# An NSA block with kc/vc projected first and its compression laid between the projection's chunks

## The reference, cut to what matters

```python
h = rms_norm(x, norm_mix[1])
q, kc, vc, ks, vs, kw, vw, gates = split(h @ nsa_w_in)       # 1024, 6 x 256, 48 columns
# compressed branch: blocks of 32 rows every 16 rows, 15 blocks, 4 groups of 64 dims
kcmp = rms_norm(silu(blocks(kc + pos_k) @ w1_k) @ w2_k, kcmp_norm)
vcmp = silu(blocks(vc + pos_v) @ w1_v) @ w2_v
o_cmp = softmax(mask(norm(q) @ kcmp.T * 0.125)) @ vcmp       # q without rope here
# two more attentions with rope(norm(q)), over (ks, vs) and (kw, vw)
x = x + (gate0 * o_cmp + gate1 * o_sel + gate2 * o_win) @ nsa_w_out
x = x + memory_cross_attention(rms_norm(x), rms_norm(mem), ...)   # its k and v come from mem
x = x + swiglu(rms_norm(x))
```

## Time and profile before

| | |
|---|---|
| three runs | 1833.73, 1836.98, 1840.62 us, median 1836.98 |
| the profiled execution | 1841.69 us, its span 1840.0 us |
| PE, DVE, ACT, POOL busy over the span | 94%, 62%, 45%, 24% |
| PE clock granted over the span | 0.956 |
| NSA block, projection (445.9 to 508.1 us) | PE full |
| NSA block, 508.1 to 580.7 us | PE granted 0.50 to 1.00 in turns |
| NSA block, attention (580.7 to 659.0 us) | granted 1.00 nearly throughout |

### The profile page before, as it was taken

One profiled execution on the slowest core, in us unless ns is written; L12 is line 12 of the kernel. 1 busy time (PEld: TensorE's weight loads), 2 busy tenths in 40 slices (PEclk: granted clock), 3 DMA queues, 4 the chain that ended last, 5 costly groups with the idle time before them and its releaser, 6 DMA issues. The chain is left out here.

```text
span 1840.0 us, 27212 instructions
## 1 busy us (share of the span) xinstructions
PE 1726.5 (94%) x11063; PEld 1544.7 (84%) x11063; DVE 1144.6 (62%) x1675; ACT 829.4 (45%) x1250; POOL 450.1 (24%) x518
## 2 busy tenths in 40 slices
PE   7899789999988997999999999999999999989998
PEld 5767679987876775999888798799988789879997
DVE  5747556554644756555456875677745787668773
ACT  5434444443432443444344335466534433646652
POOL 1600100001440001000025960224403594223430
PEclk9978899999977998999999899999999999999999
DMA  7501246655520023565655343476556534257652
GB/s 251 179 24 48 93 134 193 183 200 162 195 87 23 24 73 107 144 189 181 203 162 182 115 138 115 115 208 183 184 183 183 160 115 138 92 149 209 185 188 73
DMA packets 293164, 265.58 MB, mean 144 GB/s; under 512 B 18608, under 2 KB 254128, under 8 KB 293040
## 3 DMA queue, kind: packets, MB, share of 16 engines
q1 hardware_dynamic: 293040, 263.85, 46.3%
HBM read 262.78 MB, written 1.05 MB: 143 GB/s over the span
## 5 line engine op out<-in xcount | busy, mean ns | idle before, releaser
L144 DVE TENSOR_TENSOR w_lo<-w_raw,w_hi 128x2048 fp32r<-128x2048 f32 (+1 forms) x246 | 565.4, 2300 | 305.3 <-ACT w_hi L143 299.3
L1506 PE MATMUL bank<-h_hi,w_hi 128*128 128x256 f32 x1984 | 567.1, 286 | 1.8 <-PEq L2029 0.6
L143 ACT ACTIVATE w_hi<-w_raw 128x2048 fp32r<-128x2048 f32 (+1 forms) x246 | 464.8, 1893 | 230.7 <-PE bank L466 128.9
L1507 PE MATMUL bank<-h_lo,w_hi 128*128 128x256 f32 x1984 | 562.6, 284 | 0.0
L1508 PE MATMUL bank<-h_hi,w_lo 128*128 128x256 f32 x1984 | 562.4, 283 | 0.0
L1506 PEld LDWEIGHTS bank<-h_hi,w_hi 128*128 128x128 f32 x1984 | 382.0, 193 | 3.6 <-issue 2.9
L1507 PEld LDWEIGHTS bank<-h_lo,w_hi 128*128 128x128 f32 x1984 | 382.1, 193 | 0.3
L1508 PEld LDWEIGHTS bank<-h_hi,w_lo 128*128 128x128 f32 x1984 | 381.9, 193 | 0.0
L396 PE MATMUL bank<-w_hi,h_hi 128*128 128x512 f32 (+3 forms) x368 | 136.2, 370 | 11.3 <-DVE w_lo L144 6.6
L398 PE MATMUL bank<-w_hi,h_lo 128*128 128x512 f32 (+3 forms) x368 | 135.0, 367 | 0.0
L397 PE MATMUL bank<-w_lo,h_hi 128*128 128x512 f32 (+3 forms) x368 | 134.9, 367 | 0.0
(11 more groups left out here) (431 smaller groups left out, 2972.8 us busy)
## 6 DMA issues: line engine op xcount, KB each, us to landing
w_raw<-in_w_in SPq DMA_DIRECT2D x48, 1024.0 KB, 5.0
w_raw<-in_ffn_w_in SPq DMA_DIRECT2D x88, 512.0 KB, 5.2
w_raw<-in_w_up SPq DMA_DIRECT2D x88, 512.0 KB, 5.2
w_raw<-in_ffn_w_out SPq DMA_DIRECT2D x22, 1024.0 KB, 4.8
w_raw<-in_w_down SPq DMA_DIRECT2D x22, 1024.0 KB, 4.9
w_raw<-in_nsa_w_in SPq DMA_DIRECT2D x10, 1024.0 KB, 5.3
w_raw<-in_ab_w_in SPq DMA_DIRECT2D x8, 1024.0 KB, 8.6
w_raw<-in_mem_w_kv SPq DMA_DIRECT2D x8, 1024.0 KB, 5.2
```

The lines of the kernel that those rows point to most:

```text
L143: return act.activation(hi, raw, ACT.Copy)
L144: return dve.tensor_tensor(self.lo[:, cut_slot, 0:k * n], raw, hi.bitcast(F32), ALU.subtract)
L1506: pe.matmul(out, h, hi[:, f, :], start=(f == 0), stop=False)
L1507: pe.matmul(out, h, lo[:, f, :], start=False, stop=False)
```

## The change

- The projection's blocks are in the order kc/vc, q, q, ks/vs, kw/vw, gates, and the callback `after` on PE comes after each chunk with its number in the block.
- On PE, after the second chunk of block 1: the transposes of kc/vc; after each chunk of block 2: one hidden layer; after the second of block 3: the second layer; after the first of block 4: `turn_q`, after the second: the turn of the compressed keys. ACT's and DVE's counterparts stand in their callbacks of blocks 1 to 4.
- The position vectors are a fifth group of `tokens` (the other columns of it zero), so that the hidden layer has 75 columns and no separate position products. `tokens` lies in the attention's buffers.
- The compressed keys are stored twice with zeros between, so that one score product over all 128 partitions serves two heads: 16 products of 32 columns instead of 32 of 16.
- After the projection: turn of the memory rows into banks 0 to 3, all scores in one bank, memory pieces 0 to 9, transposes of the probabilities, pieces 10 to 15, output products, pieces 16 to 31, feature turn, attention without pieces. The four groups of pieces go to banks 0, 1, 2, 3. The softmax is made once for both row tiles.
- POOL doubles kc/vc first, and makes the compressed key's factor ahead of the third and fourth head norm and of all ropes. The scaling of the kw segment on DVE moves behind the softmax.

The diff, cut to its core (leading blanks shortened; of the queues only the added and unchanged lines, what they replace is in the listing above):

```diff
@@ Project.pe
-            if after is not None:
-                after(pe, j)
+                if after is not None:
+                    after(pe, j, c - self.first[j])
@@ MemoryRows.pe
+            g = i // 8
+            if f == 0 and g >= len(self.sums):
+                pe.wait_ge(self.copied, g - len(self.sums) + 1)
...
+            bank = self.k.bank[self.sums[g % len(self.sums)]][:, :]
@@ nsa_first
-    return [c for col in (0, 512) for c in column_chunks(a["nsa_w_in"], C_W, KD, col, 512)]
+    return [c for col in (C_KC, C_Q) for c in column_chunks(a["nsa_w_in"], C_W, KD, col, 512)]
@@ block_nsa
+tokens = free(k.att[:, :, :, :], [[(NG + 1) * S, 2], [S, NG + 1], [1, S]])
+cmp_pf = [k.exps[:, t, :].rearrange("p (g q) -> p g q", g=NG) for t in range(T)]
+blocks = [(c, c, min(512, C_W - c)) for c in (C_KC, C_Q, C_Q + 512, C_KS, C_KW, C_G)]
@@ gpsimd
+pool.wait_ge(cmp_in, 16 * 5)
+pool.tensor_copy(free(tokens[:, :, :, :], [[(NG + 1) * S, 2], [2, 16]], NG * S), pos_cols[:, :, :])\
+    .then_inc(const, 1)
+pool.wait_ge(project.copied_a, 1)
+pool.wait_ge(project.copied_d, 1)
+copy_twice(pool, scaled, 0, C_KC, ct_doubled)
+copy_twice(pool, scaled, 4, C_VC, ct_doubled)
 pool.wait_ge(gains_in, 16)
 hn.pool(pool, 0)
+mem.features.factors(pool, 2)
 hn.pool(pool, 1)
 pool.wait_ge(ck_stat, 1)
 pool.tensor_scalar(cmp_stat[:, 1:2], cmp_stat[:, 0:1], 1.0 / HD, EPS, ALU.mult, ALU.add)\
     .then_inc(ck_rstd, 1)
 pool.wait_ge(ck_rstd, 1)
 pool.tensor_tensor(cmp_stat[:, 2:3], cmp_stat[:, 1:2], k.minus_half(1), ALU.pow).then_inc(ck_rstd, 1)
+hn.pool(pool, 2)
+pool.wait_ge(turn_q.turned, 4)
+hn.pool_rope(pool, 0)
+hn.pool(pool, 3)
+hn.pool_rope(pool, 1)
+for i in (2, 3):
+    hn.pool_rope(pool, i)
+    pool.wait_ge(hn.turned, hn.turns[i])
+    copy_twice(pool, double[:, :, :, :].rearrange("p t s c -> p t (s c)"), 4 * (i - 2),
+               C_KS if i == 2 else C_KW, doubled)
@@ scalar
+def compress(act, j):
     for i, seg in enumerate(segments):
         if seg[5] == j:
             act.wait_ge(project.copied_a, j + 1)
...
             hn.act(act, i)
     if j == 1:
         mem.act_square(act)
+        for b in range(4):
+            act.wait_ge(ct_turned, b + 1)
+            act.activation(tokens[0:HD, b // 2, 2 * (b % 2):2 * (b % 2) + 2, :],
+                           k.bank[4 + b][0:HD, :].rearrange("p (a b) -> p a b", b=S), ACT.Copy)\
+               .then_inc(ct_low, 1)
+    if j == 2:
+        for i in range(2):
+            act.wait_ge(ch_sum, i + 1)
+            act.activation(cmp_bias[:, i:i + 1], k.bank[HIDDEN[i]][0:HD, NG * N_CMP:NG * N_CMP + 1],
+                           ACT.Copy).then_inc(ch_bias, 1)
+        for i in range(2):
+            act.wait_ge(ch_bias, i + 1)
+            act.wait_ge(const, 7)
+
+            to = hid[0][:, :, 0:N_CMP] if i == 0 else hid[1][:, :, :, 0:N_CMP]
+            of = [[N_CMP, NG], [1, N_CMP]] if i == 0 else [[N_CMP, NG], [0, 4], [1, N_CMP]]
+            act.activation(to, free(k.bank[HIDDEN[i]][0:HD, :], of), ACT.Silu,
+                           bias=cmp_bias[:, i:i + 1]).then_inc(ch_hid, 1)
+    if j == 3:
+        act.wait_ge(ck_out, 1)
+        act.activation(cmp_k[:, 0, :], k.bank[6][:, 0:HD], ACT.Square, accum_out=cmp_stat[:, 0:1])\
+           .then_inc(ck_stat, 1)
+        turn_q.act(act)
+    if j == 4:
+        act.wait_ge(ck_turned, 1)
+        act.wait_ge(const, 8)
+        for part in range(2):
+            rows_ = slice(HD * part, HD * part + HD)
+            act.activation(cmp_kf[rows_, :, part, :], free(k.bank[KEYS][rows_, :], [[32, NG], [1, 16]]),
+                           ACT.Copy).then_inc(ck_feat, 1)
+
+project.act(act, compress)
 mem.features.round(act, range(KD))
+act.wait_ge(cs_step, 4)
+e = probs[:, :, :, 0:16]
+act.activation(e, e, ACT.Exp).then_inc(cs_exp, 1)
 mem.act(act, 0)
 act.activation(proj[:, :, C_G:C_G + 48], proj[:, :, C_G:C_G + 48], ACT.Sigmoid).then_inc(gates, 1)
+act.wait_ge(cp_turned, 2)
+act.activation(cmp_pf[1], k.bank[TURNED[1]][:, :].rearrange("p (g q) -> p g q", g=NG), ACT.Copy)\
+   .then_inc(cp_copied, 1)
 mem.act(act, 1)
 mem.act_next(act, 1)
+mem.act(act, 2)
+mem.act_next(act, 2)
+mem.act(act, 3)
 turn.act(act)
+att.act(act)
 turn_out.act(act)
@@ vector
+def compress(dve, j):
     for i, seg in enumerate(segments):
+        if seg[5] == j - 1 and j < 5:
             hn.dve_scale(dve, i)
     for i, seg in enumerate(segments):
         if seg[5] == j:
             hn.dve_sum(dve, i)
+    if j == 1:
+        for b in range(4):
+            dve.wait_ge(ct_turned, b + 1)
+            dve.tensor_copy(tokens[HD:P, b // 2, 2 * (b % 2):2 * (b % 2) + 2, 0:S - 1],
+                            free(k.bank[4 + b][HD:P, :], [[S, 2], [1, S - 1]], 1)).then_inc(ct_high, 1)
+    if j == 3:
+        dve.wait_ge(const, 14)
+        dve.wait_ge(ck_out, 1)
+        dve.wait_ge(ck_rstd, 2)
+        dve.scalar_tensor_tensor(out=cmp_k[:, :, :], in0=free(k.bank[6][:, :], both),
+                                 scalar=cmp_stat[:, 2:3], in1=free(g(1), both), op0=ALU.mult,
+                                 op1=ALU.mult).then_inc(ck_key, 1)
+        dve.wait_ge(cv_out, 1)
+        for grp in range(NG):
+            dve.tensor_tensor(cmp_v[:, grp, :, :], free(k.bank[7][:, :], [[0, 4], [1, HD]], HD * grp),
+                              free(own[:, :], [[1, 4], [0, HD]]), ALU.mult).then_inc(cv_own, 1)
+        turn_q.dve(dve)
+
+project.dve(dve, compress)
+mem.features.cut(dve, range(4))
+e = probs[:, :, :, 0:16]
+row = lambda i: soft[:, i, :].rearrange("p (t h) -> p t h", t=T)
+wide = lambda v: free(v, [[NH, T], [1, NH], [0, 16]])
+dve.wait_ge(cs_scores, 1)
+for t in range(T):
+    dve.scalar_tensor_tensor(out=probs[:, t, :, 0:16], in0=free(k.bank[SCORES][:, :], [[16, NH], [1, 16]], S * t),
+                             scalar=0.125, in1=free(cmp_mask[:, t, :], [[0, NH], [1, 16]]), op0=ALU.mult,
+                             op1=ALU.add).then_inc(cs_step, 1)
+dve.wait_ge(cs_step, 2)
+dve.tensor_reduce(row(0), e, AX.X, ALU.max).then_inc(cs_step, 1)
+dve.wait_ge(cs_step, 3)
+dve.tensor_tensor(e, e, wide(row(0)), ALU.subtract).then_inc(cs_step, 1)
+mem.features.cut(dve, range(4, KD))
+dve.wait_ge(cs_exp, 1)
+dve.tensor_tensor(e, e, free(cmp_keep[:, :, :], [[16, T], [0, NH], [1, 16]]), ALU.mult).then_inc(cs_step, 1)
+dve.wait_ge(cs_step, 5)
+dve.tensor_reduce(row(1), e, AX.X, ALU.add).then_inc(cs_step, 1)
+dve.wait_ge(cs_step, 6)
+dve.tensor_scalar(row(2), row(1), TINY, None, ALU.max).then_inc(cs_step, 1)
+dve.wait_ge(cs_step, 7)
+dve.reciprocal(row(3), row(2)).then_inc(cs_step, 1)
+dve.wait_ge(cp_turned, 1)
+dve.tensor_copy(cmp_pf[0], k.bank[TURNED[0]][:, :].rearrange("p (g q) -> p g q", g=NG))\
+   .then_inc(cp_copied, 1)
+hn.dve_scale(dve, 3)
 mem.dve(dve, 0)
+dve.wait_ge(cs_step, 8)
+dve.wait_ge(gates, 1)
+dve.tensor_tensor(row(2), row(3), free(proj[:, :, :], [[C_W, T], [3, NH]], C_G), ALU.mult)\
+   .then_inc(cs_step, 1)
+dve.wait_ge(cs_step, 9)
 for t in range(T):
     dve.wait_ge(co_out, t + 1)
     for half in range(2):
         dve.tensor_tensor(
             out[:, t, 512 * half:512 * half + 512].rearrange("p (h d) -> p h d", d=HD),
             k.bank[OUTPUT[t][half]][:, :].rearrange("p (h d) -> p h d", d=HD),
+            free(soft[:, 2, :], [[1, 8], [0, HD]], NH * t + 8 * half), ALU.mult).then_inc(co_stored, 1)
+mem.dve(dve, 1)
+mem.dve(dve, 2)
 turn.dve(dve)
 dve.wait_ge(hn.sums, len(segments))
+dve.wait_ge(co_stored, 2 * T)
+att.dve(dve, finish)
 turn_out.dve(dve)
@@ tensor
+def hidden(pe, i):
+    if i == 0:
+        pe.wait_ge(ct_low, 4)
+        pe.wait_ge(ct_high, 4)
+        pe.wait_ge(const, 15)
+        pe.wait_ge(cmp_in, 16 * 5)
+    for c in range(16):
+        ins = pe.matmul(k.bank[HIDDEN[i]][0:HD, 0:(NG + 1) * N_CMP], w1[:, i, c, :],
+                        free(tokens[:, i, :, :], [[S, NG + 1], [16, N_CMP]], 2 * c),
+                        start=(c == 0), stop=(c == 15))
+    ins.then_inc(ch_sum, 1)
+
+def compress(pe, j, half):
+    if (j, half) == (1, 1):
+        pe.wait_ge(ct_doubled, 4)
+        for b in range(4):
+            for c in range(2):
+                for t in range(T):
+                    ins = pe.transpose(k.bank[4 + b][:, c * S + t * P:c * S + (t + 1) * P],
+                                       scaled[:, t, P * (2 * b + c):P * (2 * b + c) + P], k.ident[:, :])
+            ins.then_inc(ct_turned, 1)
+    if j == 2:
+        hidden(pe, half)
+    if (j, half) == (3, 1):
+        pe.wait_ge(ch_hid, 1)
+        pe.matmul(k.bank[6][:, 0:HD], hid[0][:, :, :], w2[:, 0, :], start=True, stop=True).then_inc(ck_out, 1)
+        pe.wait_ge(ch_hid, 2)
+        for grp in range(NG):
+            ins = pe.matmul(k.bank[7][:, HD * grp:HD * grp + HD],
+                            hid[1][:, grp, :, :], w2[:, 1, :], start=True, stop=True)
+        ins.then_inc(cv_out, 1)
+    if (j, half) == (4, 0):
+        pe.wait_ge(ck_key, 1)
+        pe.wait_ge(cv_own, NG)
+        turn_q.pe(pe, lambda pe, i: pe.wait_ge(hn.gained, i // 4 + 1))
```

(27 more changed lines are left out.)

209 lines of the change are left out of this document (20 added, 189 removed).

## The result

The changed kernel takes 1863.7 us (median of 4 runs, 1859.42 to 1866.61) against 1838.6 us beside it: ratio 1.0143, 95% interval 1.0119 to 1.0166. It is 1.4% slower, where 1821.7 us (about 1% faster) was forecast. The profiled execution has a span of 1862.7 us.

What follows compares the result with a forecast made beforehand. Bound taken: TensorE's queue plus its waits between projection and attention, 150.9 us before. Terms 20.3 + 11.2 + 28.6 + 4.8 + 26.7 + 44.1 = 135.7, 15.2 less, at full clock: 1821.7 us at the median's level, 8-in-10 range 1809 to 1835.

Runs made afterwards that it cites:

- experiment 4: 24 spare 512-column matmuls in one run between feature turn and attention, added to the changed kernel: 1866.83 us, ratio 1.0153.

## What to carry to other kernels

Before work is taken out of a latency-bound loop, list the gaps it was filling on TensorE, whose granted clock changes: a gap's price can be not its length but the time until the clock comes back, here the whole rest of the attention. Put independent work where the gaps of 1 us and more are (here the first round, in which nothing else is in flight, and the rounds behind a finish), and a few pieces may do. If a long stretch stays at half clock, one unbroken run of transposes or wide matmuls behind its last long gap is worth trying (a run of 8 us gave back 34 here, 27 net); ahead of the gap, as in experiment 4, it was lost.
